# Gate-up weights of an expert in one 2 MB transfer, issued after the whole gate-up product, in place of two halves of 1 MB

## The reference

```python
# router: top-1 of 4 groups, then top-2 of the 8 experts in it; comb holds each token's two weights
for gi in range(N_GROUPS):
    gate, up = jnp.split(jnp.einsum('nd,edf->nef', t, w_gu[gi]), 2, axis=-1)
    hmid = jax.nn.silu(gate) * up * comb[:, gi, :, None].astype(t.dtype)
    out = out + jnp.einsum('nef,efd->nd', hmid, w_dn[gi])
```

## Time and profile before

| | us |
|---|---|
| median of 3 runs (lowest, highest) | 547.43 (545.36, 549.88) |
| the profiled execution: time | 548.79 |
| the profiled execution: span from first to last instruction | 547.0 |
| PE busy | 469.1 (86%) |
| DVE busy | 194.8 (36%) |
| ACT busy | 109.3 (20%) |
| mean granted TensorE clock | 0.915 |

### The profile page before, as it was taken

One profiled execution on the slowest core, in us unless ns is written; L12 is line 12 of the kernel. 1 busy time (PEld: TensorE's weight loads), 2 busy tenths in 40 slices (PEclk: granted clock), 3 DMA queues, 4 the chain that ended last, 5 costly groups with the idle time before them and its releaser, 6 DMA issues.

```text
span 547.0 us, 6888 instructions
## 1 busy us (share of the span) xinstructions
PE 469.1 (86%) x2711; PEld 271.0 (50%) x2711; DVE 194.8 (36%) x571; ACT 109.3 (20%) x237; POOL 27.6 (5%) x55
## 2 busy tenths in 40 slices
PE   4999999999996999999569999789895999597370
PEld 4556546566665667766467556254531535152120
DVE  1300002424427335452642842334350525223234
ACT  4113112111112625424401101001010101010004
POOL 4000020000005010001000000001000000000000
PEclk8899999999998799989759998879997999889785
DMA  8997810000009612000713999999999999999802
GB/s 277 367 387 198 325 61 20 2 0 0 1 12 406 255 40 78 20 1 1 305 42 110 427 410 415 418 415 421 411 420 412 421 415 419 418 417 418 322 2 116
DMA packets 37978, 131.36 MB, mean 240 GB/s; under 512 B 10090, under 2 KB 10134, under 8 KB 29752
## 3 DMA queue, kind: packets, MB, share of 16 engines
q1 hardware_dynamic: 36672, 127.12, 59.2%
q10 hardware_dynamic: 664, 2.14, 1.0%
q0 software_dynamic: 608, 1.62, 0.8%
HBM read 127.68 MB, written 3.19 MB: 239 GB/s over the span
## 4 chain that ended last, share of the span: by engine, by line
PE 62%; DMA 24%; SPq 6%; DVE 4%; issue 2%; ACT 2%; DVEq 0%; ACTq 0%
PE bank L1432 59%; DMA gu_ring<-in_w_expert_gate_up 18%; DMA dn_ring<-in_w_expert_down 4%; SPq L523 2%; DMA gu_ring<-in_w_in 2%; SPq L526 1%; PE bank L1632 1%; PE bank L1551 1%; DVE X L1420 1%; SPq L535 1%; ACT r_xT L925 1%; DVE pnorm L1039 1%; PE bank L1602 0%; SPq L532 0%; DVE r_qz L1125 0%
## 5 line engine op out<-in xcount | busy, mean ns | idle before, releaser
L1432 PE MATMUL bank<-gu_ring,r_xT 128*32 128x512 f32 (+1 forms) x560 | 86.9, 659 | 26.6 <-DMA gu_ring<-in_w_expert_gate_up 26.5
L1432 PEld LDWEIGHTS bank<-gu_ring,r_xT 128*32 128x32 f32 (+1 forms) x560 | 28.3, 127 | 82.1 <-issue 81.9
L1432 PE MATMUL bank<-r_xT,gu_ring 128*128 128x384 f32 x192 | 65.2, 498 | 1.6 <-DMA gu_ring<-in_w_in 1.6
L1432 PEld LDWEIGHTS bank<-BT,r_qz 128*128 128x128 f32 x384 | 46.3, 202 | 10.5 <-issue 10.5
L1432 PE MATMUL bank<-BT,r_qz 128*128 128x128 f32 x384 | 47.8, 288 | 4.2 <-DVE BT L1230 4.2
L1432 PEld LDWEIGHTS bank<-r_xT,gu_ring 128*128 128x128 f32 x192 | 37.0, 195 | 27.1 <-DMA gu_ring<-in_w_in 1.9
L1432 PE MATMUL bank<-r_xs 128*128 128x512 f32 x96 | 49.5, 645 | 0.0
L1432 PE MATMUL bank<-r_xT,dn_ring 128*128 128x384 f32 x128 | 42.6, 486 | 0.0
L1308 DVE TENSOR_TENSOR X<-X,bank 128x512 f32<-128x512 f32 x48 | 33.0, 687 | 23.0 <-PE bank L1432 22.5
L1432 PE MATMUL bank<-dn_ring,V 128*32 128x512 f32 x256 | 30.5, 619 | 7.3 <-ACT V L871 3.9
L1278 DVE TENSOR_SCALAR r_kT<-r_kT 128x256 f32<-128x256 f32 x8 | 2.4, 294 | 87.5 <-ACT r_kT L861 87.5
(11 more groups left out here) (289 smaller groups left out, 506.1 us busy)
## 6 DMA issues: line engine op xcount, KB each, us to landing
gu_ring<-in_w_expert_gate_up SPq DMA_DIRECT2D x64, 1024.0 KB, 18.8
dn_ring<-in_w_expert_down SPq DMA_DIRECT2D x32, 1024.0 KB, 20.3
gu_ring<-in_w_in SPq DMA_DIRECT2D x4, 2048.0 KB, 12.2
dn_ring<-in_w_in SPq DMA_DIRECT2D x2, 2048.0 KB, 19.2
gu_ring<-in_w_out SPq DMA_DIRECT2D x2, 2048.0 KB, 9.4
r_xs<-in_cache_k SPq DMA_DIRECT2D x8, 256.0 KB, 10.0
r_xs<-in_cache_v SPq DMA_DIRECT2D x8, 256.0 KB, 6.2
X<-in_x SPq DMA_DIRECT2D x3, 512.0 KB, 4.1
```

Source lines behind the costliest of these rows:

```text
L1432: return te.matmul(out, lhsT, rhs, start=start, stop=stop, **kw)
```

## The change

load_up sends an expert's whole gate-up matrix (2 MB, 16 KB for each partition) by one instruction. For n from 1 on all four are issued after gu_full, that is when both halves of gate_up(n-1) are done; the wait on gu_mid and the semaphore itself are gone. ld_gu has one semaphore for a slot, and gate_up(n) waits for all four before its first half. load_down, the spare expert's loads and every other engine stay as they are.

```diff
-        ld_gu = [[sem(f"ld_gu{half}{i}") for i in range(RING)] for half in range(2)]
+        ld_gu = [sem(f"ld_gu{i}") for i in range(RING)]
...
-            def load_up(n, h, half):
-
-                ks = slice(half * HALF_K * 2 * F, (half + 1) * HALF_K * 2 * F)
-                sp.dma_start(gu_ring[:, h, ks], w_gu[n * WIDE + h][:, ks]).then_inc(ld_gu[half][h], 16)
+            def load_up(n, h):
+
+                sp.dma_start(gu_ring[:, h, :], w_gu[n * WIDE + h]).then_inc(ld_gu[h], 16)
...
             sp.wait_ge(g_full, g_of["B", CT - 1] + 1)
-            for half in range(2):
-                for h in (2, 3):
-                    load_up(0, h, half)
+            for h in (2, 3):
+                load_up(0, h)
...
             sp.wait_ge(g_full, g_of["oA", TT - 1, 1] + 1)
-            for half in range(2):
-                for h in (0, 1):
-                    load_up(0, h, half)
+            for h in (0, 1):
+                load_up(0, h)
             for n in range(1, QUADS):
-                sp.wait_ge(gu_mid, n)
-                for h in range(WIDE):
-                    load_up(n, h, 0)
                 sp.wait_ge(gu_full, n)
                 for h in range(WIDE):
-                    load_up(n, h, 1)
+                    load_up(n, h)
                 sp.wait_ge(y_full, n)
                 for h in range(WIDE):
                     load_down(n, h)
...
                 for half in range(2):
                     pe.wait_ge(xgt_evac, n * 2 + (half + 1))
-                    for h in range(WIDE):
-                        pe.wait_ge(ld_gu[half][h], n * 16 + 16)
+                    if half == 0:
+                        for h in range(WIDE):
+                            pe.wait_ge(ld_gu[h], n * 16 + 16)
...
-                    ins.then_inc(gu_full if half else gu_mid, 1)
+                ins.then_inc(gu_full, 1)
```

More of the change, by code:

```diff
@@ L363, in build @@
         xgt_evac = sem("xgt_evac")
-        gu_mid = sem("gu_mid")
         gu_full = sem("gu_full")
```

## The result

The changed kernel takes 1.0262 times the time of the one before (95% interval 1.0219 to 1.0305), medians 564.24 and 547.21 us over six executions each. The medians hold every execution, while the ratio leaves out two of the changed kernel (568.07 and 571.26 us) that ran in a slower state, over 1.5% above its fastest; by the ratio the change costs 14.3 us. The forecast was 12.6. The profiled execution took 565.2 us with a span of 563.5, against 548.79 and 547.0: a span 16.5 us longer.

The account below looks back on a forecast made before the run. Weight transfers bound the experts' stretch. Start 3.5, bubbles 7.4, less 1.4 for an irregular step, and end 3.1 make +12.6 us: median 547.43 becomes 560.0, 2.3% more; forecast 555 to 564 (65%), range 550.5 to 569.

Parts of the forecast that it names:

- the cover of D(n): Experts' stretch: a step's down weights land 10.05 us after its gate-up weights; the next gate-up weights must be issued before.
- Part 1: Start of the stream: step 1's gate-up weights are all issued only when gate_up(0) ends, landing later; +3.5 us.
- Part 2: gate_up after a wait: at the low clock the whole takes 9.2 us, against 7.07 at full clock.
- Part 3: Experts' steps: gaps in the stream ahead of the gate-up weights of steps 3, 4, 5 and 7, 1.85 us each, 7.4 us.
- the irregular step: Kernel before, last step to U(7)'s landing: 31.5 us instead of 30.1; its 1.4 us were not carried over.
- rival 2: Experts' stretch: a restart costs more than 2.5 us, 4.0 at worst, with five bubbles; 567 to 576 us; 15%.
- its bound of 0.3 us a step: Gate-up transfers: 16 KB pieces were taken to change nothing, with 0.3 us a step, 2 us in all, as bounds.
- The claim that a wait of some 2 us is safe: Ahead of gate_up(5): 2.2 us of idling was to leave TensorE's clock up, so no bubble ahead of step 6's gate-up weights.
- Part 4: End, step 7: a whole gate_up follows the last gate-up landing, so down(7) starts later; +3.1 us.
- The Trainium skill's fixed 2.0 us for each transfer: Transfers: not seen in the pace, so halving their count gives nothing; at a restart it would make bubbles 0.5 us smaller.
- the row's 2.5 us: Restart of the stream after a stretch without traffic: 2.5 us from issue, beside the transfer's own bytes.
- Rival 1: Experts' steps: the clock stays up or returns early, the cover holds, no bubbles; 551.1 us, within 1%; 17%.

Follow-up runs that it names:

- e10: Changed kernel with 768 KB more to move behind the down weights of steps 3 to 6; 1.0329 of the kernel before.
- e11: Kernel before with the same extra 768 KB in each of steps 3 to 6, nothing else changed; 1.0193 of the kernel before.
- e1: Kernel before with the first gate-up halves too issued after gu_full, TensorE still waiting by half; 1.0046 of the kernel before.
- e4: Kernel before with gate_up waiting for all eight weight halves before its first half, issue and sizes kept; 1.0039 of the kernel before.
- e7: Changed kernel with step 1's gate-up weights in halves, issued at gu_mid and gu_full as before, full wait kept; 1.0242 of the kernel before.
- e12: The changed kernel measured once more, beside other runs on one chip; 1.0276 of the kernel before.
- e2: Changed kernel with each 2 MB gate-up transfer as two of 1 MB, late issue and full wait kept; 1.0372 of the kernel before.
- e8: Changed kernel with step 7's gate-up weights in halves, both issued after gu_full, and TensorE waiting by half there; 1.0231 of the kernel before.
- e5: Kernel before with halves of two experts in one 2 MB transfer, 8 KB pieces, schedule and waits kept; 0.9983 of the kernel before.
- e9: Changed kernel with 2 to 8 unused matmuls keeping TensorE at work in each wait ahead of gate_up in steps 1 to 7; 1.0079 of the kernel before.

## Why the prediction held

**The stream bounds the stretch, and what keeps it going is that U(n+1) is issued under the cover of D(n).** Right; e10 and e11 show it from the side of the stream, e1 and e4 show that either half of the change alone leaves the cover whole.

**Part 1, 3.5 us.** 3.4 in the trace of the changed kernel at U(1) (29.5 for 26.1 from gate_up(0)), 3.1 at U(2). e7 takes it away in the trace.

**Part 2, gate_up 9.2 us.** Measured 8.73, 9.55, 10.03, 8.77 and 8.45 in steps 2 to 6, mean 9.1, 9.46 in step 1, and 9.72 in step 7, where I had 8.67.

**Part 3, 7.4 us of bubbles.** Less the 1.4 of the irregular step that makes 6.0 from U(2) to U(7); measured 9.8, and 9.1 in e12's trace. Two terms were small.

The first is the traffic of a step behind a restart, 2.2 us in all over the steps ahead of U(3), U(4), U(5) and U(7). From first issue to last landing a step's gate-up weights took 23.6, 23.4, 22.6, 22.8 and 22.9 us, mean 23.1, where 2.5 + 20.1 was taken. The restart is only part of it: the first 2 MB landed 7.5 to 8.1 us after their issue, which with 4.9 for the bytes is a restart of 2.9 on the mean and not 2.5; rival 2, whose mechanism this is, had 4.0. The rest is that in steps 3, 4 and 7 one transfer in the middle of the stream landed about 1 us late (for U(3) see the rows above); e2's trace has it in the same three steps. What holds that transfer up is not shown. In the kernel before, the irregular step has one too: of D(6), the first, issued at 462.16, landed at 480.4, and the second, issued at 462.58, at 484.1, 3.7 us later, where down matrices follow one another at 2.5 to 2.6.

```profile
dn_ring<-in_w_expert_down SPq DMA_DIRECT2D x1, 1024.0 KB, 18.2
...
dn_ring<-in_w_expert_down SPq DMA_DIRECT2D x1, 1024.0 KB, 21.5
```

So 1.2 of the 1.4 us that the forecast took off are one such late transfer, and the changed kernel has its own. Against all this goes the faster pace of 16 KB pieces, 2.45 us for 1 MB where 2.49 was the pace before: the prediction took nothing for it, and its bound of 0.3 us a step is what it gave.

The second is step 5, 1.7 us: 2.17 us of idling was to leave the clock up, but gate_up(5) took 8.77. The windows there (columns as above) show the clock going down when TensorE was at work again, from 457.49 on:

```profile
456.00:457.00 1.00, 0.00 (x0) 0.00 (x0) 0.05 (x1) 0.00 (x0) 0.00 (x0) 1.00 0.85 348
457.00:458.00 1.00, 0.51 (x8) 0.26 (x12) 0.00 (x0) 0.00 (x0) 0.00 (x0) 0.97 1.03 426
458.00:459.00 1.00, 1.00 (x12) 0.42 (x8) 0.00 (x0) 0.00 (x0) 0.00 (x0) 0.50 1.01 406
```

The claim that a wait of some 2 us is safe rested on one row and failed: in step 5 e2, e7 and e12 took 8.8 us after 2.0 us of idling, e8 took 7.1 after 1.96 and e10 after 2.58. A wait of that length can go either way.

**Part 4, 3.1 us.** 4.2, of which 1.05 is gate_up(7) at its longer time; 0.9 more came behind it, in down(7) itself (5.91 for 5.02). In e12's trace it is 2.6, with gate_up(7) at 8.36. e8 gives back 3.1 us against the first trace, 1.5 against the second.

**The Trainium skill's fixed 2.0 us for each transfer** ("DMA: Bandwidth & Descriptors", section "Anatomy of one DMA"). The section gives it for transfers that GpSimd issues, while SyncE issues these, and puts it down mostly to the completion of the transfer, so it is no gap between transfers that follow one another. As a cost of each transfer it does not show here: e5 halves the count of transfers in the full stream and gains nothing, e2 doubles the changed kernel's and its landings take 0.3 us a step longer for four more, which the pieces account for. For the restart, the row's 2.5 us was nearer than 2.0 to the 2.9 measured.

**Rival 1** was priced at 551.1 if the clock stayed up. e9 keeps the clock up, and its ratio on the median before is 551.5. Its steps are still 0.6 us longer than the 30.1 of that rival: by the landings there is a gap of 0.3 to 1.1 us behind D(2), D(3) and D(5), none behind D(4) and D(6), and here too single transfers came late. With a restart of 2.9 us the cover just comes out even, and the 0.25 us of margin are gone. That the same kernel moves from one case to the other by the clock alone is the best evidence for the mechanism.

**The sum.** It is 1.7 us short of the timed runs (14.3 against 12.6; the interval is 12.0 to 16.7). Against the traces it is shorter: from the start of gate_up(0) to the end, the changed kernel takes 18.1 us more than the kernel before in the first profiled execution and 15.1 in e12's. So the mechanism and the places of the loss were right, but that the timed result came this close is in part luck, with step 5 and the traffic behind a restart both counted too low.

## What to carry to other kernels

In a stream that bounds a kernel, write down for each transfer how long after the previous landing it is issued and how many bytes are queued ahead of it then: here 10 us of cover less a whole gate_up and less the restart came out about even at full clock (0.25 us to spare by the forecast, none in e9) and 2 us short at the low one, while with half a gate_up ahead of the issue (e1, e4) the stream did not break. Work that starts behind a wait of 5 us or more is to be counted at the low clock, here 2 us on 7.1 (1.4 to 3.0), and the transfer issued at its end pays for that. Splitting a buffer's release in two costs a few instructions and buys half of the work as margin; fewer transfers bought nothing once 1 MB transfers stood in a full queue, and pieces of 16 KB in place of 8 bought 0.3 us on 8 MB.

## What the runs showed of the hardware

- Transfers that fill 64 of 128 partitions moved 215 GB/s with the transfer engines busy at 1.02; in the full stream those of 128 partitions moved 410 to 430. I had expected the same pace.
- The clock can fall while TensorE is at work again: it had been idle 2.17 us before 457.49, and the granted clock went from 1.00 to 0.50 between 457 and 458. After 0.23 to 1.94 us of idling, in e9, it stayed up each time.
- Pieces of 16 KB moved 2 MB in 4.90 us in a full stream (U(2) of the changed kernel), pieces of 8 KB in 4.97, whether in one transfer (e5) or in two (before).
- In the stream single transfers land about 1 us late, in steps 3, 4 and 7 of the changed kernel and of e2, and at D(6) before. No run shows why.
